# A fused decoder trunk on one core: the first feed forward pair multiplied on the scaled x1, with norm factor and shift put in behind PSUM

## The reference, cut to what matters

```
x = x + g1 * mixer(h)                                   # called x1 here
h = rmsnorm(x, norm2_g) * (1 + sc2) + sh2
x = x + g2 * ((silu(h @ w1) * (h @ w3)) @ w2)           # hidden width 2816
```

## Time and profile before

| | us |
|---|---|
| median of 3 runs (862.41 to 865.15) | 864.17 |
| the profiled execution | 864.41 |
| its span on the core | 862.7 |
| PE busy | 837.3 (97%) |
| DVE busy | 441.9 (51%) |
| ACT busy | 322.1 (37%) |
| POOL busy | 45.7 (5%) |

### The profile page before, as it was taken

How to read it: one execution, slowest core, us unless ns; L and a number is a source line. 1 busy time by engine, 2 the same in 40 slices (tenths; PEclk the granted TensorE clock), 3 DMA queues, 4 the chain that set the end, 5 groups by cost and what they waited for, 6 DMA issues and landing times.

```text
span 862.7 us, 10537 instructions
## 1 busy us (share of the span) xinstructions
PE 837.3 (97%) x3932; PEld 677.0 (78%) x3932; DVE 441.9 (51%) x713; ACT 322.1 (37%) x475; POOL 45.7 (5%) x74
## 2 busy tenths in 40 slices
PE   5999999999999899999999999999999999999996
PEld 3587888877787678878888788888888888888886
DVE  6789977247678764335863553333333333223222
ACT  4535545342323444442334543333333332222231
POOL 5300000000000000000002100000000000000110
PEclk9999999999999999998999999999999999999999
DMA  9843223348775121124323233333333332323322
GB/s 349 264 85 98 73 74 94 88 147 289 248 269 171 49 73 51 50 74 147 97 86 117 67 98 98 97 97 97 97 95 95 94 95 88 107 86 95 105 68 97
DMA packets 149372, 100.67 MB, mean 117 GB/s; under 512 B 11072, under 2 KB 142552, under 8 KB 148312
## 3 DMA queue, kind: packets, MB, share of 16 engines
q1 hardware_dynamic: 149128, 100.14, 38.5%
q10 hardware_dynamic: 208, 0.05, 0.0%
HBM read 97.03 MB, written 2.10 MB: 115 GB/s over the span
## 4 chain that ended last, share of the span: by engine, by line
PE 86%; DVE 6%; DMA 3%; ACT 2%; issue 1%; SPq 1%; DVEq 0%; ACTq 0%
PE bank L1701 25%; PE bank L1703 25%; PE bank L1702 25%; DMA raw<-in_w_in 3%; PE bank L1848 1%; PE bank L1944 1%; PE bank L1868 1%; PE bank L1879 1%; DVE wlo L1188 1%; PE bank L1969 1%; PE bank L1923 1%; PE bank L1935 1%; ACT whi L698 1%; PE bank L1920 0%; SPq L454 0%
## 5 line engine op out<-in xcount | busy, mean ns | idle before, releaser
L1701 PE MATMUL bank<-h_lo,whi 128*128 128x512 f32 x712 | 284.7, 400 | 1.7 <-DVE wlo L1185 0.8
L1703 PE MATMUL bank<-h_hi,wlo 128*128 128x512 f32 x712 | 278.0, 390 | 0.0
L1702 PE MATMUL bank<-h_hi,whi 128*128 128x512 f32 x712 | 277.8, 390 | 0.0
L1701 PEld LDWEIGHTS bank<-h_lo,whi 128*128 128x128 f32 x712 | 134.2, 189 | 35.6 <-issue 7.1
L1703 PEld LDWEIGHTS bank<-h_hi,wlo 128*128 128x128 f32 x712 | 134.0, 188 | 28.8
L1702 PEld LDWEIGHTS bank<-h_hi,whi 128*128 128x128 f32 x712 | 134.3, 189 | 27.8 <-issue 1.2
L698 ACT ACTIVATE whi<-raw 128x1024 fp32r<-128x1024 f32 x60 | 63.3, 1057 | 163.7 <-PE bank L1703 123.3
L1188 DVE TENSOR_TENSOR wlo<-raw,whi 128x1024 fp32r<-128x1024 f32 x60 | 73.3, 1223 | 99.5 <-ACT whi L698 99.3
L1703 PE MATMUL bank<-a_hi,wlo 128*128 128x512 f32 x176 | 68.5, 389 | 0.0
L1701 PE MATMUL bank<-a_lo,whi 128*128 128x512 f32 x176 | 68.5, 389 | 0.0
L1702 PE MATMUL bank<-a_hi,whi 128*128 128x512 f32 x176 | 68.5, 389 | 0.0
(11 more groups left out here) (335 smaller groups left out, 990.1 us busy)
## 6 DMA issues: line engine op xcount, KB each, us to landing
raw<-in_ffn_w SPq DMA_DIRECT2D x60, 512.0 KB, 3.8
raw<-in_w_in SPq DMA_DIRECT2D x44, 512.0 KB, 4.1
slab<-in_mod_w SPq DMA_DIRECT2D x32, 512.0 KB, 5.7
modA<-in_mod_w SPq DMA_DIRECT2D x4, 1024.0 KB, 11.6
modB<-in_mod_w SPq DMA_DIRECT2D x4, 1024.0 KB, 18.3
raw<-in_w_out SPq DMA_DIRECT2D x8, 512.0 KB, 3.6
raw<-in_ffn_w SPq DMA_DIRECT2D x8, 384.0 KB, 3.3
xtok<-in_x SPq DMA_DIRECT2D x4, 512.0 KB, 5.8
```

Source lines behind the costliest of these rows:

```text
L1701: mm(dst, w_h, m_l, start=first, stop=False)
L1702: mm(dst, w_h, m_h, start=False, stop=False)
L1703: return mm(dst, w_l, m_h, start=False, stop=last)
```

## The change

The first pair (chunks 61 and 62) is no longer multiplied with h but with `z`, x1 times the channel scale. The token's norm factor is one number per column of the result and is multiplied in afterwards; the shift sh2 gives one number per output channel, sh2 @ w, and is added last. In detail:

- ACT writes, for every block of x1, beside `x1g` also its rounded form `z_hi`, right after the block's square; DVE takes the low part `z_lo` a block later.
- DVE sums shift times weight over the 8 blocks of channels for each of the two chunks (`shift_times_w`, 8 linked steps of 128x128 into `sacc`), before the low part replaces the raw weights; PE sums `sacc` over the partitions by one column product each (bank 6), and DVE copies the two columns to `bcol`.
- PE multiplies the first pair (banks 4 and 7) right behind w_out. The square sums stand behind its third block, the broadcast (now bank 5) and the column products behind its fifth. All three `keep_clock` calls there are gone. ACT copies the broadcast rows to SBUF (`rbs`), and `htmp` is made from them.
- The blocks of h feed only chunks 63 and 64 (banks 2 and 3), two at a time. Their weights are converted ahead of the blocks of h; in the kernel before, chunk 63 was converted between them by DVE and chunk 64 behind them.
- DVE multiplies the banks of the first pair by `rbs` (`zt`), ACT makes silu(zt + bcol), DVE (zt + bcol) times it. The first turn of the loops on ACT and DVE is written out for this, with the weights of chunks 65 to 68 converted in it.

The diff, without the new semaphores:

```diff
+        z_hi = at("z_hi", [P, KB, L], F32R, 83)
+        z_lo = at("z_lo", [P, KB, L], F32R, 99)
+        rbs = at("rbs", [P, L], F32, 139)
+        sacc = at("sacc", [P, 2, P], F32, 141)
+        bcol = at("bcol", [P, 2], F32, 142)
+        zt = at("zt", [P, 2, L], F32, 143)
...
+            def scaled(n):
+                if n == 0:
+                    act.wait_ge(s_gs2, 1)
+                    act.wait_ge(s_x2t, KB)
+                    act.wait_ge(s_up, 3 * KB)
+                A(z_hi[:, n], xT[:, n], ACT.Copy, scale=gs2[:, n:n + 1]).then_inc(s_zhi, 1)
+                A(x1g[:, n], xT[:, n], ACT.Copy, scale=gs2[:, n:n + 1]).then_inc(s_x1g, 1)
...
                     A(sq[:, n % 2], xT[:, n], ACT.Square).then_inc(s_sq, 1)
-            def scaled(n):
-                A(x1g[:, n], xT[:, n], ACT.Copy, scale=gs2[:, n:n + 1]).then_inc(s_x1g, 1)
-            act.wait_ge(s_gs2, 1)
-            act.wait_ge(s_x2t, KB)
+                    scaled(n)
+            def hi4(s, need):
+                act.wait_ge(w_loaded[s % 4], SLOT_LOADS[s])
+                act.wait_ge(w_mm, need)
+                A(whi4[:, s % 4], raw[:, s % 4], ACT.Copy).then_inc(w_hi, 1)
...
-            for n in range(S_F1 - 3 - S_OUT):
-                scaled(n)
             for n in range(S_F1 - 3 - S_OUT, KB):
+                act.wait_ge(s_col, n + 1)
                 if n == KB - 1:
-                    act.wait_ge(w_mm, S_F1 - 1)
-                    for s in range(S_F1, S_F1 + 2):
-                        act.wait_ge(w_loaded[s % 4], SLOT_LOADS[s])
-                        A(whi4[:, s % 4], raw[:, s % 4], ACT.Copy).then_inc(w_hi, 1)
-                act.wait_ge(s_col, n + 1)
+                    scaled(n)
...
                 A(sq[:, n % 2], xT[:, n], ACT.Square).then_inc(s_sq, 1)
-                scaled(n)
+                if n < KB - 1:
+                    scaled(n)
+                if n == KB - 3:
+                    hi4(S_F1, S_F1 - 2)
+                    hi4(S_F1 + 1, S_F1 - 1)
+            hi4(S_F1 + 2, S_F1)
             act.wait_ge(s_sqmm, 1)
             A(rstd[:], ps[5][:, 0:NT], ACT.Sqrt, bias=epst[:, 0:1], scale=1.0 / D).then_inc(s_std, 1)
-            act.wait_ge(w_loaded[(S_F1 + 2) % 4], SLOT_LOADS[S_F1 + 2])
-            A(whi4[:, (S_F1 + 2) % 4], raw[:, (S_F1 + 2) % 4], ACT.Copy).then_inc(w_hi, 1)
+            hi4(S_F1 + 3, S_F1)
+            act.wait_ge(s_rb, 1)
+            A(rbs[:], ps[5][:], ACT.Copy).then_inc(s_rbs, 1)
             for k in range(KB):
...
                 if k in H2_POOL:
...
-            s = S_F1 + 3
-            act.wait_ge(w_loaded[s % 4], SLOT_LOADS[s])
-            act.wait_ge(w_mm, S_F1)
-            A(whi4[:, s % 4], raw[:, s % 4], ACT.Copy).then_inc(w_hi, 1)
+            for s in range(S_F1 + 4, S_F1 + 6):
+                hi4(s, s - 3)
+            act.wait_ge(s_zt, 1)
+            act.wait_ge(s_shb, 1)
+            A(sil[:, 0], zt[:, 0], ACT.Silu, bias=bcol[:, 0:1]).then_inc(s_sil, 1)
+            act.wait_ge(s_act, 3)
+            A(a_hi[:, 0], aa[:, 0], ACT.Copy).then_inc(s_ahi, 1)
+            act.wait_ge(w_mm, S_F1 + 3)
+            A(sil[:, 1], ps[2][:], ACT.Silu).then_inc(s_sil, 1)
+            act.wait_ge(s_act, 4)
+            A(a_hi[:, 1], aa[:, 1], ACT.Copy).then_inc(s_ahi, 1)
+            for s in range(S_F1 + 6, S_F1 + 8):
+                hi4(s, s - 3)
             def silu_pair(i, u):
...
+                dve.wait_ge(s_zhi, n + 1)
+                V.scalar_tensor_tensor(out=z_lo[:, n], in0=xT[:, n], scalar=gs2[:, n:n + 1],
+                                       in1=z_hi[:, n].bitcast(F32), op0=ALU.mult, op1=ALU.subtract
+                                       ).then_inc(s_zlo, 1)
             for t in range(1, S_F1):
...
+                    if n:
+                        scaled_lo(n - 1)
             def lo4(s):
...
+            def shift_times_w(w):
+                s = S_F1 + w
+                dve.wait_ge(w_loaded[s % 4], SLOT_LOADS[s])
+                dve.wait_ge(s_late, 3)
+                for k in range(KB):
+                    if k == 0:
+                        ins = V.tensor_scalar(sacc[:, w], raw[:, s % 4, k], modc[:, 24:25], None, ALU.mult)
+                    else:
+                        ins = V.scalar_tensor_tensor(out=sacc[:, w], in0=raw[:, s % 4, k],
+                                                     scalar=modc[:, 24 + k:25 + k], in1=sacc[:, w], op0=ALU.mult,
+                                                     op1=ALU.add)
+                    if k < KB - 1:
+                        link(ins)
+                ins.then_inc(s_shw, 1)
             for n in range(S_F1 - 3 - S_OUT, KB):
-                if n == KB - 1:
-                    lo4(S_F1)
-                    lo4(S_F1 + 1)
                 dve.wait_ge(w_mm, S_OUT + n + 1)
                 residual(n, n % 2, 16)
+                scaled_lo(n - 1)
+                if n == KB - 3:
+                    shift_times_w(0)
+                    dve.wait_ge(s_shw, 1)
+                    lo4(S_F1)
+                    shift_times_w(1)
+                if n == KB - 2:
+                    dve.wait_ge(s_shw, 2)
+                    lo4(S_F1 + 1)
+            scaled_lo(KB - 1)
+            lo4(S_F1 + 2)
             def h2_lo(k):
...
             V.reciprocal(rstd[:], rstd[:]).then_inc(s_rr, 1)
-            dve.wait_ge(s_rb, 1)
+            lo4(S_F1 + 3)
+            dve.wait_ge(s_rbs, 1)
             for k in range(KB):
...
                 if k >= 4:
...
-                V.tensor_tensor(htmp[:, k % 4], x1g[:, k], ps[3][:], ALU.mult).then_inc(s_h2, 1)
+                V.tensor_tensor(htmp[:, k % 4], x1g[:, k], rbs[:], ALU.mult).then_inc(s_h2, 1)
                 if k and k - 1 not in H2_POOL:
...
-                if k == 1:
-                    lo4(S_F1 + 2)
+                if k == 5:
+                    dve.wait_ge(s_shc, 1)
+                    V.tensor_copy(bcol[:], ps[6][:, 0:2]).then_inc(s_shb, 1)
             h2_lo(KB - 1)
-            lo4(S_F1 + 3)
+            for w in range(2):
+                dve.wait_ge(w_mm, S_F1 + w + 1)
+                V.tensor_tensor(zt[:, w], ps[(4, 7)[w]][:], rbs[:], ALU.mult).then_inc(s_zt, 1)
+            lo4(S_F1 + 4)
+            dve.wait_ge(s_sil, 1)
+            dve.wait_ge(s_zt, 2)
+            V.scalar_tensor_tensor(out=aa[:, 0], in0=zt[:, 1], scalar=bcol[:, 1:2], in1=sil[:, 0], op0=ALU.add,
+                                   op1=ALU.mult).then_inc(s_act, 1)
+            dve.wait_ge(s_act, 3)
+            dve.wait_ge(s_ahi, 1)
+            V.tensor_tensor(a_lo[:, 0], aa[:, 0], a_hi[:, 0].bitcast(F32), ALU.subtract).then_inc(s_alo, 1)
+            lo4(S_F1 + 5)
             def act_product(n, u, dst):
...
-                    if n == KB - 1 and k == KB - 2:
-                        pe.wait_ge(s_x2c, KB)
-                        pe.wait_ge(s_sqa, KB - 2)
-                        square_columns(sqa, True)
                     if n == 0:
...
-            keep_clock(3)
-            pe.wait_ge(s_sq, KB)
-            square_columns(sq[:, (KB - 1) % 2], False).then_inc(s_sqmm, 1)
-            keep_clock(1)
-            pe.wait_ge(s_rr, 1)
-            for t in range(NT):
-                ins = mm(ps[3][:, t * P:(t + 1) * P], rstd[:, t:t + 1].broadcast_to([P, P]), ident[:],
-                         start=True, stop=True)
-            ins.then_inc(s_rb, 1)
-            keep_clock(4)
-            pe.wait_ge(w_lo, S_F1 + 2)
+            for k in range(KB):
+                pe.wait_ge(s_zlo, k + 1)
+                for w in range(2):
+                    s = S_F1 + w
+                    if k == 0:
+                        pe.wait_ge(w_lo, s + 1)
+                    ins = split_mm(ps[(4, 7)[w]][:], whi4[:, s % 4, k], wlo[:, s % 4, k], z_hi[:, k], z_lo[:, k],
+                                   k == 0, k == KB - 1)
+                    if k == KB - 1:
+                        ins.then_inc(w_mm, 1)
+                if k == 2:
+                    pe.wait_ge(s_x2c, KB)
+                    pe.wait_ge(s_sqa, KB - 2)
+                    square_columns(sqa, True)
+                    pe.wait_ge(s_sq, KB)
+                    square_columns(sq[:, (KB - 1) % 2], False).then_inc(s_sqmm, 1)
+                if k == 4:
+                    pe.wait_ge(s_rr, 1)
+                    for t in range(NT):
+                        ins = mm(ps[5][:, t * P:(t + 1) * P], rstd[:, t:t + 1].broadcast_to([P, P]), ident[:],
+                                 start=True, stop=True)
+                    ins.then_inc(s_rb, 1)
+                    pe.wait_ge(s_shw, 2)
+                    for w in range(2):
+                        ins = mm(ps[6][:, w:w + 1], sacc[:, w], ones[:, 0:1], start=True, stop=True)
+                    ins.then_inc(s_shc, 1)
             for k in range(KB):
                 if k in H2_POOL:
...
-                for w in range(3):
-                    s = S_F1 + w
-                    if k == 0 and w == 2:
+                for w in range(2):
+                    s = S_F1 + 2 + w
```

(9 more changed lines are left out.)

15 lines of the change are left out of this document (13 added, 2 removed).

## The result

The changed kernel takes 857.97 us, median of 8 runs (855.77 to 859.99), beside 862.82 for 8 runs of the kernel before (861.52 to 866.17, the three shown earlier among them). The ratio is 0.9946, 95% interval 0.9929 to 0.9962: 4.7 us faster, 3.3 to 6.1. The profiled execution took 858.89 for a span of 857.2; before it was 864.41 for 862.7. One later run of the kernel before, taken with experiments 1 to 4, lasted 2160.20 us and counts as slow; it is left out of every ratio and median here. The ratios are the recorded ones, not quotients of two medians; the two differ by up to 0.0015.

The account below looks back on a forecast made before the run. PE, holding 86% of the chain that ended last, was taken as the bound. Gain 4.9 - 0.8 - 0.2 = 3.9 us gave 860.5 from the profiled execution, 860.3 from the 0.24 lower median; range 858.2 to 863.2.

Parts of the forecast that it names:

- The stretch: PE from the last six w_out products to the feed forward loop's first product: 31.35 us before the change.
- Without waits: Same PE stretch after the change if PE never waits: 26.49 us, a gain of 4.9.
- Norm's chain costs nothing: Between broadcast and first product of h: 2.9 us of norm work hidden behind PE's products, with 1.7 to spare.
- First wait: PE at the second weights, late because POOL's sum of squares stalls DVE's shift sums: 0.8 us, bounds nothing and 2.1.
- The prediction's pattern for it: Earlier trace: an h_lo took 1.24 instead of 0.75 us beside POOL's operation of 494.02, read as waiting for POOL.
- Second wait: PE at the loop's first product, waiting for the product aa of block 0: 0.2 us, bounds 0 to 0.6.
- The rival with both upper ends: Waits of 2.1 at the second weights and 0.6 at the loop, some 0.3 more in blocks: gain 1.9, 862.3; 15%.
- The clock rival: Without fillers PE's clock falls behind the wait at the second weights: 8.4 us lost, 868.7; 4%.
- the level: Starting time of the kernel before from which the gain was subtracted: 864.17 us, median of its runs.
- Numbers: Part setting the range: runs of before spread 862.41 to 865.15, so a median can sit 0.9 to either side.
- The low end: Lower limit of the forecast range: 859.3 - 1.1 = 858.2 us.
- the best case: Rival that PE has no wait at all, at the second weights or the loop: gain 4.9, 859.3 us; 25%.

Follow-up runs that it names:

- experiments 1 to 4: Kernel before without its fillers, 865.45 us; changed kernel with POOL's block 5 sum held back, 857.10; changed kernel repeated, 858.89; kernel before repeated, 861.11.
- Experiments 2 and 8: Changed kernel with POOL's block 5 sum held until the second weights are converted, 857.10 us; changed kernel without 14 of 16 shift-sum steps, 856.47 us.
- experiment 6: Changed kernel with one more ACT operation of 0.61 us ahead of the first silu: 858.01 us, ratio 0.9955.
- experiment 1: Kernel before without the 8 fillers behind w_out, nothing else changed: 865.45 us, ratio 1.0033.
- experiment 3: Changed kernel run again unaltered, for its trace, against the kernel before: 858.89 us, ratio 0.9952.

## Why the prediction was right or wrong

**The stretch.** Predicted 27.49 (26.49 and 1.0 of waits), measured 27.18; the gain 3.9 against 4.17 in the stretch and 4.3 in the tail. By its terms:

- Without waits: 26.49 predicted, 27.18 - 0.80 = 26.38 measured. Squares, broadcast and columns took 0.81 + 0.89 + 0.89 + 0.36 = 2.95 where 3.06 were costed; of the three slow first products only two show.
- Norm's chain costs nothing: right. The first h_lo ended at 495.44, TensorE wanted it at 496.95: 1.5 in hand, where 1.7 was predicted.
- First wait: 0.8 predicted, 0.80 measured. The cause was right, that the sizes agree is partly luck: the step counted one wait of 0.9 at full length, and the trace shows one of 0.53 with 0.27 of restart around it. The cause in detail: counted from block 5's update the conversion ends at 12.0 (predicted 12.3) and TensorE is there at 11.4 (predicted 11.4). POOL held the chain for 3.73 - 2.68 = 1.05 where I had taken 1.2; steps without it go 0.385 apart. Experiments 2 and 8 each take it away and gain 0.84 and 0.9. (The prediction's pattern for it, in the earlier trace rows, is POOL's low part of a block of h at 494.02 and not a sum of squares, as it is called there; the reading of its end holds.)
- Second wait: 0.2 predicted, nothing measured. Of the bounds 0 to 0.6 the lower one came, by 0.19 us; experiment 6 shows that this margin is real. The times added up there, 15.1 to 15.6 against 15.5, give a wait of 0.1 at most; the other 0.5 of the upper bound was an allowance for POOL.
- The rival with both upper ends needed the second POOL sum ahead of the last conversion, an order of two queues 0.2 apart by my times. They came 0.17 apart, in the order of the forecast and not of the rival: DVE's conversion started first, at 482.11, and kept its 1.22, POOL's sum started at 482.28 and took 2.20 instead of 1.29. With so narrow a distance that is a good part luck.
- The clock rival: the mechanism is in the kernel before (experiment 1), but not in the new stretch, at 1.00 throughout.

**The number.** The step that failed is the level, a term of the sum that was mis-sized: it was taken at 864.17, the median of three runs, and under **Numbers** "a median can sit 0.9 to either side" was to cover its error. That median stood 1.35 above the one of all eight runs (862.82), and later sets of 21, 25, 11 and 10 runs of the same kernel gave 862.50, 862.69, 863.10 and 863.06. Of all threes that can be drawn from the set of 25, 36% have a median over 0.9 from 862.69, 23% one over 0.9 above it. The low end was moreover set 1.1 below the best case, 859.3, and not 0.9, and even this was too little. The miss of 2.3 us is then: 1.35 of level, 0.4 of gain (4.3 instead of 3.9), and 0.55 by which the eight runs of the changed kernel fell low too, which I put down to chance: with the eleven more of experiment 3 its median is 858.52, inside the range. As a ratio the forecast, 3.9 of 864.17 or 0.9955, lies in the measured interval.

The warning stood in the rows: the 0.50 of the earlier trace rows and products 0.42 apart were a fall of the clock in the execution that I was reading. Its way from 385.4 to block 0's update took 62.2 us; in the 13 other traces it took 59.4. I read the rows as an example of what could happen behind the change, and not as 2.8 us that the next execution would not have. What raised the median of the three other runs is not shown: they left no trace. The two profiled executions differ by 1.2 us ahead of the change for this: before lost 2.8 at 386, after 1.6 at 354.
